# Order of two matmul groups at the ends of seven softmax attentions in a two-block transformer kernel

## What is computed

```python
# moba, per head: causal
p = softmax(q @ k.T + causal); o = p @ v
# diff, per head, two comps c of 64: causal with a relative bias
p = softmax(q_c @ k_c.T * scale + bias); attn = p_0 - lam * p_1; o = attn @ v
# cross, 4 heads of 256, not causal
logits = einsum('bshd,bmhd->bhsm', q, k) * CA_HEAD_DIM ** -0.5
p = jax.nn.softmax(logits, axis=-1)
o = jnp.einsum('bhsm,bmhd->bshd', p, v).reshape(B, S, D_MODEL)
x = x + o @ w_o
```

## Time and profile before

| | |
|---|---|
| time, median of 3 runs | 2690.26 us (2688.77 to 2692.3) |
| the profiled execution's own time | 2689.89 us |
| its span | 2688.1 us |
| PE busy | 2516.8 us, 94% |
| PE weight load busy (beside PE) | 1885.3 us, 70% |
| DVE busy | 1314.2 us, 49% |
| ACT busy | 1068.5 us, 40% |
| POOL busy | 59.7 us, 2% |
| mean granted clock of TensorE | 0.97 of full speed |
| HBM traffic | 203 GB/s over the span |

### The profile page before, as it was taken

The page is one execution under the profiler, slowest core; times in us unless marked ns, Lnnn a source line. Parts: engine busy times, 40 slices in busy tenths (PEclk is TensorE's granted clock), DMA queues, the critical chain, the costliest instruction groups (busy, mean ns, idle before and its releaser), DMA issues.

```text
span 2688.1 us, 33869 instructions
## 1 busy us (share of the span) xinstructions
PE 2516.8 (94%) x11962; PEld 1885.3 (70%) x11962; DVE 1314.2 (49%) x1930; ACT 1068.5 (40%) x1627; POOL 59.7 (2%) x86
## 2 busy tenths in 40 slices
PE   8998988898988799999999899999999999899998
PEld 6875433586432478878778787887787887788886
DVE  5644111463111566455555555554556555654654
ACT  4442111352110454444444344444444444544443
POOL 0000000000000100000000000000000000000000
PEclk9998999898999899999999999999999999899999
DMA  7547999547999434365543054654455554353652
GB/s 240 180 164 288 362 409 409 210 136 285 391 409 409 168 129 143 131 210 186 175 133 126 10 195 134 211 187 163 157 173 174 188 190 138 116 167 123 225 186 97
DMA packets 149969, 546.14 MB, mean 203 GB/s; under 512 B 17032, under 2 KB 17233, under 8 KB 149721
## 3 DMA queue, kind: packets, MB, share of 16 engines
q1 hardware_dynamic: 144664, 526.04, 55.0%
q0 software_dynamic: 4912, 17.43, 2.1%
q10 hardware_dynamic: 272, 1.05, 0.1%
HBM read 543.39 MB, written 2.63 MB: 203 GB/s over the span
## 4 chain that ended last, share of the span: by engine, by line
PE 76%; DMA 10%; DVE 6%; ACT 3%; issue 2%; POOL 1%; SPq 0%; DVEq 0%; POOLq 0%; ACTq 0%
PE bank L1908 20%; PE bank L1910 19%; PE bank L1909 19%; DMA stage_w<-in_wide 5%; DMA pair_w<-in_wide 5%; PE bank L2157 4%; PE bank L1986 2%; PE bank L2183 2%; DVE low_w L1074 2%; PE bank L2435 1%; PE bank L2481 1%; PE bank L2497 1%; PE bank L2405 1%; DVE y L1128 1%; ACT tmp L911 1%
## 5 line engine op out<-in xcount | busy, mean ns | idle before, releaser
L1908 PE MATMUL bank<-high_w,xh 128*128 128x512 f32 x2112 | 850.3, 403 | 29.1 <-DVE low_w L1074 11.4
L1074 DVE TENSOR_TENSOR low_w<-stage_w,high_w 128x1024 fp32r<-128x1024 f32 x528 | 641.0, 1223 | 400.4 <-ACT high_w L671 374.2
L1910 PE MATMUL bank<-high_w,xl 128*128 128x512 f32 x2112 | 831.7, 394 | 0.0
L1909 PE MATMUL bank<-low_w,xh 128*128 128x512 f32 x2112 | 831.4, 394 | 0.0
L671 ACT ACTIVATE high_w<-stage_w 128x1024 fp32r<-128x1024 f32 x528 | 554.6, 1059 | 205.8 <-PE bank L1910 183.3
L1908 PEld LDWEIGHTS bank<-high_w,xh 128*128 128x128 f32 x2112 | 402.3, 190 | 126.1 <-issue 32.7
L1910 PEld LDWEIGHTS bank<-high_w,xl 128*128 128x128 f32 x2112 | 401.9, 190 | 86.8
L1909 PEld LDWEIGHTS bank<-low_w,xh 128*128 128x128 f32 x2112 | 403.1, 191 | 79.3
L1412 DVE TENSOR_TENSOR qk<-qk,bank 128x256 f32<-128x256 f32 x32 | 13.5, 422 | 270.4 <-ACT qk L801 270.4
L1908 PE MATMUL bank<-high_d,hidden_h 128*128 128x512 f32 x320 | 124.9, 390 | 0.0
L1910 PE MATMUL bank<-high_d,hidden_l 128*128 128x512 f32 x320 | 124.6, 389 | 0.0
(11 more groups left out here) (286 smaller groups left out, 2715.9 us busy)
## 6 DMA issues: line engine op xcount, KB each, us to landing
stage_w<-in_wide SPq DMA_DIRECT2D x592, 512.0 KB, 4.5
pair_w<-in_wide SPq DMA_DIRECT2D x128, 512.0 KB, 14.6
stage_d<-in_down SPq DMA_DIRECT2D x120, 512.0 KB, 4.3
proj<-in_wide SPq DMA_DIRECT2D x64, 512.0 KB, 14.2
pair_d<-in_down SPq DMA_DIRECT2D x64, 512.0 KB, 12.9
proj<-in_down SPq DMA_DIRECT2D x32, 512.0 KB, 12.1
gain<-in_gains POOLq DMA_DIRECT2D x19, 512.0 KB, 4.8
skew<-bias_dram POOLq DMA_DIRECT2D x1, 1536.0 KB, 16.8
```

Of the source, the lines that this page charges most:

```text
L1074: vec.tensor_tensor(low_w[:, w], stage_w[:, w], high_w[:, w].bitcast(F32), ALU.subtract)\
L1908: pe.matmul(o, hi, wh, start=start, stop=False)
L1909: pe.matmul(o, hi, wl, start=False, stop=False)
L1910: return pe.matmul(o, lo, wh, start=False, stop=stop)
```

## The change

Three edits, all in PE's `attention`:

- In a step with no value pieces, in moba and diff, `head(j - 2)` stands ahead of `turn_probs(j - 1)`. These are steps 6 and 7.
- Behind the last step, in all seven attentions, `head(H - 2)` stands ahead of `turn_probs(H - 1)`.
- Cross keeps its order inside the steps, although its step 3 has no value pieces.

No instruction is added, removed or resized, no semaphore wait is added or dropped, and the other engines' streams are the same; PE's waits move with the groups they belong to.

```diff
@@ -2447,12 +2447,15 @@
                     for c in range(C):
                         scores(C * j + c)
                     fill(each[j])
+                    ahead = s.which != "cross" and not each[j]
+                    if ahead:
+                        head(j - 2)
                     if j:
                         turn_probs(j - 1)
-                    if j >= 2:
+                    if j >= 2 and not ahead:
                         head(j - 2)
+                head(H - 2)
                 turn_probs(H - 1)
-                head(H - 2)
                 turn_half(after(s), 0)
                 head(H - 1)
```

## The result

The changed kernel takes 2698.68 us (median of 7, 2694.92 to 2701.71), the kernel before 2689.83 us (median of 7 in the same comparison, 2679.38 to 2695.38). The ratio is 1.0038, 95% interval 1.0021 to 1.0055: slower by 0.4%. The profiled execution of the changed kernel took 2694.92 us (span 2693.1), the fastest of its seven, so it shows 5.0 us of the loss, and not 8.8.

A forecast was written before the change was run, and what follows sets the result against it. PE was taken to bound the kernel, 76% of the chain. Cross +1.7, moba +1.0 and diff -0.6 made +2.1 us on the profiled 2689.89, thus 2692.0, or 2692.4 as a median; range 2689.0 to 2697.5.

The forecast's parts named there:

- Rival 1: Moba and cross ends: longer idle times lower the clock, 1.7 us per stretch, slower by over 0.2%, up to 2697.5; chance 0.15.
- What bounds, and which group is ready first: PE is 76% of the chain; at stage ends the turn is ready first in cross and moba, the product in diff.
- Cross, the turn: Four cross ends: the turn moves behind the product and delays what follows by 0.43 us each, +1.7 us in all.
- Moba: Moba's end: step 6 costs 0; in step 7 a new PE wait for ACT's copy delays the projection, +1.0 us.
- Diff: Two diff ends: the earlier product starts the turned half 0.34 us sooner, until DVE's normalization limits; -0.3 each, -0.6 us.
- The clock: Cross and moba ends: low stretches cost 1.7 us each, which end gets one looks like chance; nothing added to the sum.
- The measurement: Whole kernel: the runs shown lie 1.5 us under their median, used for the range's lower end of 2689.0.

The follow-up runs named there:

- the change again: The changed kernel, unaltered, run a second time against the kernel before: 2697.43 us against 2689.93, ratio 1.0031.
- filled: Changed kernel plus 12 useless PE transposes of the identity in idle time at each cross end, against the kernel before: 2692.09 us against 2687.59, ratio 1.0018.
- diff alone: Kernel before with the new order only in the two diff attentions, against the kernel before: 2685.00 us against 2689.93, ratio 0.9989.
- pure delay: Kernel before plus 18 useless PE transposes behind the second cross attention's last product, against the kernel before: 2688.48 us against 2687.59, ratio 1.0008.
- moba alone: Kernel before with the new order only in moba (three swaps), against the kernel before: 2687.64 us against 2689.93, ratio 0.9997.

## Why the prediction was wrong

The forecast was +2.1 us, a range up to 2697.5 and 0.80 for no measurable change. The result was +8.8 us, outside the range on the high side. Rival 1, with 0.15, came true in its size (slower by over 0.2%) and in its cause at the cross ends; its own 2697.5 was still too low, because it had no cost in untouched stages and put one of its stretches in moba, where none came.

**What bounds, and which group is ready first: right.** The product in cross starts right behind ACT's copy, the turn was in a gap that the product could not have used, and in diff the product was ready first. All of it reads in the timelines above.

**Cross, the turn: right.** 0.43 us per end forecast. Measured at equal clock: +0.43 (first end, the change again, low clock in both kernels), +0.45 (fourth end, likewise), +0.53 and +0.48 (filled, none low).

**Moba: right.** +1.0 forecast, +0.92 to +0.94 measured. The idle time ahead of the product of head 6 is 0.64 us, forecast 0.6 to 0.7, and the swap in step 6 cost nothing. The delay was passed on.

**Diff: right for the turned half, wrong for what comes of it.** The turned half starts 0.33 us earlier against the normalization, as forecast. At the start of the projection 0.11 us is left, because the low clock covers more of what follows, which I had set at 0.04. From one normalization to the next nothing is left (at the second end 7.58 us before, 2345.69 to 2353.27; 7.61 after, 2350.22 to 2357.83). The forecast was -0.3 per end down to the second turned half. From the first normalization to the projection behind that half it was 9.8 to 10.1 us in 12 ends with the old order, and with the new order (diff not filled) 9.6 to 9.8 in six ends and 10.7 in four, both of diff alone among them. So an end gained up to 0.3 us or lost 0.9, by where the low clock fell. In the profile of the change again the two ends give -0.3 and 0.0 over this stretch.

**The clock: this step failed.** The words were "which end gets one looks like chance, since two of four did", and the idle time "grows by about 2 us of 170"; so the forecast's sum had this term at nothing. I read the second sentence as evidence against rival 1. The right comparison was local: the idle time just ahead of the work, 1.86 us against 2.35, and what the granted clock does right behind it. With 2.35 us it fell in 12 ends of 13, with 1.86 in 7 of 19. That gives (12/13 - 7/19) x 4 ends x 1.65 us = +3.7 us that the forecast did not have. "Two of four" was no chance either: with 1.86 us the first and fourth end fell in 7 of 10 cases and the second and third in 0 of 9. But that could not be read from the one profile that I had. The rule of the Trainium skill that I set beside it ("TensorE: Matmul & The Clock Gate", "A second HAM failure mode: psum-queue depth-cycling") tells of a kernel in which PE's small idle times between groups of matmuls come often enough for the clock to oscillate. Here each end has one such idle time, and the traces agree as far as that goes: low stretches followed it in these counts. I gave it too little.

**A term that was missing.** None of my cases had a cost in stages that the change doesn't touch. The pure delay shows one: 2 us later, the stage start near 1860 us has a longer low stretch, +0.87. With the third cross end late too the one near 2250 us adds +1.05. Even 0.5 us late is enough for +1.2 at each. With 1.9 us from these, 3.7 from the ends, 1.8 for the turns, 0.9 for moba and about -0.3 for diff, the sum is 8.0 us; the medians are 8.8 and 7.5 apart.

**The measurement.** I took 1.5 us for the scatter, from three runs. Thirty runs of the same kernel ranged over 10.7 us.

Still open: why diff alone is 4.9 us under before, and whether moba alone, 2.3 us under by the medians, is under it at all. The profile of before has a low stretch at the first and at the fourth cross end, 1.7 us each; diff alone has neither, moba alone has the fourth. That fits, but I have one profile of each, and the other executions of before may differ. What in the chip moves the low stretches was not tested, nor why the first and fourth end fall more readily than the second and third.

## What to carry to other kernels

When two groups compete for an idle gap, put the one that is ready first into it, and read its readiness from the engine that releases it: here ACT's copy stands behind the exponentials, so the turn fits in front. Price a longer idle time ahead of matmuls by what the granted clock does right behind it, end by end, and not by its share of the span. Where PE must wait, useless transposes in the gap can be worth more than a better order: 6.6 us here, from cross alone, and nothing more from diff. And look for the cost of a delay also in the stages behind it: a low stretch there can grow though nothing in them was changed.

## What I had not expected of the hardware

- The low clock is not spread by chance over equal places. The cross ends fell to 1.2 GHz in 12 of 13 cases with 2.35 us of idle time ahead of the last group, in 7 of 19 with 1.86 us (all at the first and fourth end), and in none of 24 once filling had cut the idle time to 1.04 or 0.55 us.
- A change of 2 us in when a place is reached changes its clock: 1.10 us for eight transposes became 1.96 with the same wait before them. All five kernels that came there 2 us late paid this 0.9 us, and none of the six that came on time.
- Executions of one unchanged kernel on one core differed by up to 15.2 us (0.6%).
